# Turning the first half of x by a transposing DMA instead of on TensorE, in front of the e block

## The reference

```python
x = first_block(x, ...)                 # ends in rms_norm(h, final_norm)
for layer in range(2):                  # second block
    h = rms_norm_2(x, g_mix[layer])
    y = even_mixer(h, e_w_in, ...)      # layer 0, "the e block": z = h @ w_in, 2568 columns
    x = x + y
    m = rms_norm_2(mem, g_mem[layer])   # the memory, 256 rows
    x = x + memory_cross_attention(rms_norm_2(x, g_xa[layer]), m, xa_wq, xa_wkv, ...)
    x = x + swiglu_2(rms_norm_2(x, g_ffn[layer]), ...)
```

## Time and profile before

| what | us |
|---|---|
| three runs, median (lowest, highest) | 1207.38 (1206.32, 1207.60) |
| the profiled execution | 1206.72 |
| its span, first to last instruction | 1204.8 |
| TensorE busy in it | 1196.0 |
| VectorE busy | 780.9 |
| ScalarE busy | 701.6 |

### The profile page before, as it was taken

The page is one execution under the profiler, slowest core; times in us unless marked ns, Lnnn a source line. Parts: engine busy times, 40 slices in busy tenths (PEclk is TensorE's granted clock), DMA queues, the critical chain, the costliest instruction groups (busy, mean ns, idle before and its releaser), DMA issues.

```text
span 1204.8 us, 16878 instructions
## 1 busy us (share of the span) xinstructions
PE 1196.0 (99%) x5622; PEld 986.7 (82%) x5622; DVE 780.9 (65%) x1107; ACT 701.6 (58%) x1030; POOL 72.5 (6%) x119
## 2 busy tenths in 40 slices
PE   9999999999999999999999999999999999999998
PEld 7888888877788888887888788888888887888887
DVE  6655655688676656557778766756566667765554
ACT  7545554666556545548676576645555546755552
POOL 0430000000000000000220110000000000000000
PEclk9999999999999999999999999999999999999999
DMA  9977754554566987756655518977655554876662
GB/s 314 275 227 232 231 171 145 170 173 131 166 196 197 280 250 228 220 148 180 201 167 171 167 61 248 267 226 206 206 156 164 160 163 148 237 231 199 202 200 76
DMA packets 218917, 234.68 MB, mean 195 GB/s; under 512 B 66608, under 2 KB 158896, under 8 KB 218864
## 3 DMA queue, kind: packets, MB, share of 16 engines
q1 hardware_dynamic: 163792, 214.61, 57.1%
q10 hardware_dynamic: 53280, 13.64, 6.2%
q0 software_dynamic: 1792, 5.75, 1.8%
HBM read 219.78 MB, written 1.05 MB: 183 GB/s over the span
## 4 chain that ended last, share of the span: by engine, by line
PE 97%; DMA 1%; DVE 1%; ACT 1%; issue 0%; ACTq 0%; DVEq 0%
PE bank L2034 30%; PE bank L2036 30%; PE bank L2035 30%; PE bank L2093 2%; PE bank L2247 1%; PE bank L2263 1%; PE bank L2234 1%; DMA sb_probs<-sb_probs 0%; DMA sb_gates<-h_xT 0%; PE bank L2232 0%; ACT sb_probs L1276 0%; PE bank L2551 0%; DVE sb_rmax L1929 0%; PE bank L2540 0%; PE bank L2265 0%
## 5 line engine op out<-in xcount | busy, mean ns | idle before, releaser
L2034 PE MATMUL bank<-sb_wh,sb_aTh 128*128 128x512 f32 (+1 forms) x1124 | 435.2, 387 | 0.7 <-DVE sb_aTl L1439 0.7
L2036 PE MATMUL bank<-sb_wh,sb_aTl 128*128 128x512 f32 (+1 forms) x1124 | 431.0, 383 | 0.0
L2035 PE MATMUL bank<-sb_wl,sb_aTh 128*128 128x512 f32 (+1 forms) x1124 | 430.7, 383 | 0.0
L1359 DVE TENSOR_TENSOR sb_wl<-sb_raw,sb_wh 128x1024 fp32r<-128x1024 f32 x269 | 325.4, 1222 | 116.5 <-ACT sb_wh L741 111.9
L741 ACT ACTIVATE sb_wh<-sb_raw 128x1024 fp32r<-128x1024 f32 (+1 forms) x275 | 284.5, 1047 | 114.5 <-PE bank L2036 24.8
L2036 PEld LDWEIGHTS bank<-sb_wh,sb_aTl 128*128 128x128 f32 x1124 | 211.2, 188 | 42.0
L2034 PEld LDWEIGHTS bank<-sb_wh,sb_aTh 128*128 128x128 f32 x1124 | 211.3, 188 | 41.7 <-DVE sb_aTl L1439 1.1
L2035 PEld LDWEIGHTS bank<-sb_wl,sb_aTh 128*128 128x128 f32 x1124 | 211.4, 188 | 40.2
L1359 DVE TENSOR_TENSOR sb_wl<-sb_z,sb_wh 128x1024 fp32r<-128x1024 f32 x132 | 160.8, 1224 | 66.7 <-ACT sb_wh L741 66.2
L741 ACT ACTIVATE sb_wh<-sb_z 128x1024 fp32r<-128x1024 f32 x132 | 138.8, 1058 | 76.0 <-PE bank L2036 68.0
L845 ACT ACTIVATE sb_junk<-bank,sb_rstd 128x256 f32<-128x256 f32 x88 | 37.0, 471 | 156.9 <-PE bank L2036 156.6
(11 more groups left out here) (220 smaller groups left out, 928.9 us busy)
## 6 DMA issues: line engine op xcount, KB each, us to landing
sb_raw<-w_in SPq DMA_DIRECT2D x80, 256.0 KB, 3.1
sb_raw<-ffn_w_down SPq DMA_DIRECT2D x60, 256.0 KB, 4.1
sb_raw<-w_down SPq DMA_DIRECT2D x60, 256.0 KB, 4.1
sb_z<-w_gate SPq DMA_DIRECT2D x52, 256.0 KB, 3.3
sb_z<-w_up SPq DMA_DIRECT2D x52, 256.0 KB, 4.1
sb_z<-ffn_w_gate SPq DMA_DIRECT2D x49, 256.0 KB, 3.6
sb_z<-ffn_w_up SPq DMA_DIRECT2D x49, 256.0 KB, 4.4
sb_raw<-e_w_in SPq DMA_DIRECT2D x40, 256.0 KB, 3.1
```

The source lines that it names most:

```text
L1359: dve.tensor_tensor(wl[:, u % NSPLIT, :], raws[SLOT[u]], wh[:, u % NSPLIT, :].bitcast(F32), ALU.subtract).then_inc(low_done, 1)
L2034: pe.matmul(dst, lh, w_hi, start=start, stop=False)
L2035: pe.matmul(dst, lh, w_lo, start=False, stop=False)
L2036: return pe.matmul(dst, ll, w_hi, start=False, stop=stop)
```

## The change

TensorE's call of `xt_half(3, 0)` goes. What ScalarE and VectorE did for the second half of x (planes of 16-bit halves, a transposing DMA, putting the halves together, high part, low part) is now done for each half on its own, with a semaphore for each DMA. The 16-bit planes of half 0 lie in `probs` and those of half 1 in `qkT[3]`; the turned planes go to `probsT` and `qkT[1]`, and the joined x to `qkT[2]` and `qkT[0]`. The lists of ScalarE and VectorE get a new order. The count of turns by TensorE before later norms falls by two (`turns_before`).

```diff
         def turns_before(norm):
-            return 4 * (norm - 1) - (2 if norm > 3 else 0)
+            return 4 * (norm - 1) - (4 if norm > 3 else 0)
...
-            def x3_split():
+            def x3_split(half):
-                act.wait_ge(x_ready, 12)
+                act.wait_ge(x_ready, 10 + 2 * half)
...
-            def x3_turn():
+            def x3_turn(half):
-                act.wait_ge(x3_planed, 1)
+                act.wait_ge(x3_planed, half + 1)
...
-            def x3_high():
+            def x3_high(half):
-                act.wait_ge(x3_joined, 1)
+                act.wait_ge(x3_joined, half + 1)
...
-            splits(mk, 4)
+            splits(mk, 3)
+            x3_split(0)
+            x3_turn(0)
+            split(mk + 3)
             rstd_known(MEM_STAT)
             evac(mk + 4, 0, MEM_STAT, kz[0], memk_evac_a)
-            x3_split()
-            xt_high(3, 0)
-            x3_turn()
+            x3_split(1)
             split(mk + 4)
+            x3_turn(1)
 
             act.wait_ge(small_in, 32)
             copy(wf_hl[:, :, 0:8], wf[:, :, :]).then_inc(wf_high, 1)
             split(mk + 5)
+            x3_high(0)
             token_ssq(3, x)
             split(mk + 6)
             head_squares(kz[0], ((memk_evac_a, 1), (memk_evac_d, 1)))
             split(mk + 7)
-            x3_high()
+            x3_high(1)
             evac(mk + 8, 2, MEM_STAT, vm[0], memv_evac_a)
...
-            xt_low(3, 0)
             split(mk + 4)
+            x3_join(0)
 
             dve.wait_ge(wf_high, 1)
             dve.tensor_tensor(wf_hl[:, :, 8:16], wf[:, :, :], wf_hl[:, :, 0:8].bitcast(F32), ALU.subtract).then_inc(wf_low, 1)
-            splits(mk + 5, 2)
+            split(mk + 5)
+            x3_low(0)
+            split(mk + 6)
             head_sums(0, 3, 4)
-            x3_join()
+            x3_join(1)
             split(mk + 7)
-            x3_low()
+            x3_low(1)
             evac(mk + 8, 2, MEM_STAT, vm[0], memv_evac_d)
...
-            chunk(mk + 4, 2, None, yTh, yTl, before={1: lambda: xt_half(3, 0)})
+            chunk(mk + 4, 2, None, yTh, yTl)
```

More of the change, by code:

```diff
@@ L234, in two_block_kernel @@
                       qkT[:, 1, :, :].rearrange("p h t -> p (h t)").bitcast(U16)]
-        x3_planes = km_planes[0]
-        x3_planesT = km_planesT[0]
-        x3T = qkT[:, 2, :, :]
+        x3_planes = [km_planes[0], qkT[:, 3, :, :].rearrange("p h t -> p (h t)").bitcast(U16)]
+        x3_planesT = [km_planesT[0], km_planesT[1]]
+        x3T = [qkT[:, 2, :, :], qkT[:, 0, :, :]]
         hT_halves = probsT[:, 0, :].bitcast(U16).rearrange("p (k t r h) -> p h k t r", k=2, t=NT, h=2)
@@ L318, in two_block_kernel @@
         x3_planed = sem("x3_planed")
-        x3_turned = sem("x3_turned")
+        x3_turned = [sem(f"x3_turned{half}") for half in range(2)]
         x3_joined = sem("x3_joined")
@@ L796, in load_tables @@
                 act.add_instruction(mybir.InstLoadActFuncSet(name=nc.get_next_instruction_name(), act_func_set_id=number))
-            def x3_split():
-                act.wait_ge(x_ready, 12)
-                halves = x[:, :, 512:1024].bitcast(U16).rearrange("p t (c h) -> p h t c", h=2)
+            def x3_split(half):
+                act.wait_ge(x_ready, 10 + 2 * half)
+                halves = x[:, :, 512 * half:512 * half + 512].bitcast(U16).rearrange("p t (c h) -> p h t c", h=2)
                 for h in range(2):
-                    ins = copy(x3_planes.rearrange("p (h t c) -> p h t c", h=2, t=NT)[:, h], halves[:, h])
+                    ins = copy(x3_planes[half].rearrange("p (h t c) -> p h t c", h=2, t=NT)[:, h], halves[:, h])
                 ins.then_inc(x3_planed, 1)
-            def x3_turn():
-                act.wait_ge(x3_planed, 1)
-                act.dma_start_transpose(x3_planesT.rearrange("p (b r) -> p b r", r=P), x3_planes).then_inc(x3_turned, 16)
-            def x3_high():
-                act.wait_ge(x3_joined, 1)
+            def x3_turn(half):
+                act.wait_ge(x3_planed, half + 1)
+                act.dma_start_transpose(x3_planesT[half].rearrange("p (b r) -> p b r", r=P), x3_planes[half]).then_inc(x3_turned[half], 16)
+            def x3_high(half):
+                act.wait_ge(x3_joined, half + 1)
                 for k in range(4):
-                    col = NORM_FILL[3][1] + 4 + k
-                    copy(aTh[:, 4 + k, :], x3T[:, k, :], vecs[:, col:col + 1]).then_inc(a_high, 1)
+                    col = NORM_FILL[3][1] + 4 * half + k
+                    copy(aTh[:, 4 * half + k, :], x3T[half][:, k, :], vecs[:, col:col + 1]).then_inc(a_high, 1)
             def km_split(l, n_normed):
@@ L1760, in _, with x3_join @@
             evac(mk + 4, 0, MEM_STAT, kz[0], memk_evac_d)
[L1762 to L1766, removed]
+            def x3_join(half):
+                dve.wait_ge(x3_turned[half], 16)
+                turned = x3_planesT[half].rearrange("p (h t k r) -> p h k t r", h=2, t=NT, k=4)
+                halves = x3T[half].rearrange("p k t -> p (k t)").bitcast(U16).rearrange("p (k t r h) -> p h k t r", k=4, t=NT, h=2)
                 for h in range(2):
@@ L1769, in x3_join, with x3_low @@
                 ins.then_inc(x3_joined, 1)
-            def x3_low():
+            def x3_low(half):
                 fill = NORM_FILL[3][0]
[L1774 to L1778, removed]
-            xt_low(3, 0)
+                for k in range(4 * half, 4 * half + 4):
+                    col = NORM_FILL[3][1] + k
+                    dve.wait_ge(a_high, 8 * fill + 1 + k)
+                    dve.scalar_tensor_tensor(aTl[:, k, :], x3T[half][:, k % 4, :], vecs[:, col:col + 1],
+                                             aTh[:, k, :].bitcast(F32), ALU.mult, ALU.subtract).then_inc(a_low, 1)
             split(mk + 4)
+            x3_join(0)
             dve.wait_ge(wf_high, 1)
             dve.tensor_tensor(wf_hl[:, :, 8:16], wf[:, :, :], wf_hl[:, :, 0:8].bitcast(F32), ALU.subtract).then_inc(wf_low, 1)
-            splits(mk + 5, 2)
+            split(mk + 5)
+            x3_low(0)
+            split(mk + 6)
             head_sums(0, 3, 4)
-            x3_join()
+            x3_join(1)
             split(mk + 7)
-            x3_low()
+            x3_low(1)
             evac(mk + 8, 2, MEM_STAT, vm[0], memv_evac_d)
```

## The result

The changed kernel takes 1211.68 us (median of six runs, 1211.06 to 1212.80) against 1207.11 us of the kernel before: 4.57 us slower, ratio 1.004 with the interval 1.003 to 1.005. A second measurement, at the end of the study, gave 1211.24 and the ratio 1.0042 (1.0028 to 1.0056). The forecast was 1208.7 with a range up to 1211.0. The sign that rival C named, an issue of over 2.4 us, is there, and the time is past the range.

The account below looks back on a forecast made before the run. TensorE, holding 97% of the chain, was taken as the bound. The sum -0.92 + 1.85 + 0.17 gave +1.1, plus 0.2 at `forget_sum`: +1.3 us, 1208.7 on the median's scale, range 1206.0 to 1211.0.

Parts of the forecast that it names:

- rival C: ScalarE's queue, planes to fourth split: closely following turns issue or fly longer; +3.3 us for the first, about +4.4 both; chance 0.21.
- The mechanism: E block's third unit: squares behind the wait for join 0 make the low parts 2.0 us late; TensorE waits 1.85 us.
- the DMA traffic: Second pass of 0.52 MB on DMA engines 98% busy: costed at nothing, the e block's splits having over 2 us cover.
- the clock: TensorE around the seam: read at full granted clock, 1.00, the 2.4 GHz level; no term for a fall.
- The saving: TensorE: eight transposes removed, worth 0.92 us, all on the path that sets the end.
- Turn 1's issue: ScalarE's queue, from 565.5 to 566.9: issue of the second transposing DMA, taken at 1.33 us rather than 3.30.
- The first unit: E block's first unit: low parts of blocks 0 to 3 in time, with 1.6 us of cover.
- `forget_sum`: Behind the e block's units: VectorE's copy for it 2.0 us late, adding 0.2 us more.
- The start after a wait: TensorE at the e block's third unit: starting after the wait costs 0.17 us more.

Follow-up runs that it names:

- no_turns_pe: Kernel before, with the eight transposes of x on TensorE left out and nothing in their place: 1206.60 us against 1206.68, ratio 0.9996.
- squares_late: Changed kernel with the two squares of x moved behind the high parts of blocks 4 to 7 on ScalarE: 1209.64 us, kernel before 1206.98.
- one_turn: Changed kernel with the second turn left out, blocks 4 to 7 joined from the first turn's data: 1209.78 us, kernel before 1206.98.
- turn1_in_halves: Changed kernel with the second turn issued as two of half the size: 1209.40 us, kernel before 1206.28.
- extra_turn_before: Kernel before, plus one full-size turn nobody uses, issued by ScalarE where the changed kernel issues its first: 1210.12 us against 1206.28.
- turn1_before_split: Changed kernel with the second turn's issue ahead of the split of the e block's first unit: 1213.42 us, kernel before 1206.68.
- turns_by_sp: Changed kernel, order kept, with both turns issued by SP between the loads of the e block's units: 1210.57 us, kernel before 1206.98.
- changed again: The changed kernel measured once more, unaltered, to see which profile rows repeat: 1211.24 us, kernel before 1206.03, ratio 1.0042.
- order_and_sp: Changed kernel with turns issued by SP and the lists in order of need, `split(mk + 5)` keeping its place: 1209.43 us, kernel before 1206.98.
- ballast3: Kernel before, with three extra VectorE subtractions in front of the low parts of blocks 4 to 7: 1211.64 us against 1206.68.

## Why the prediction was wrong

The mechanism was right, and the sum was short. It put the DMA traffic at nothing, where a late load cost 1.3 us; it took the shorter of two rows for the second issue, where the longer cost 0.6 us; and it had no term for the clock, which cost 1.4 us.

- **The saving (-0.92).** The term was read rightly from the rows, but it is gross. Taken alone it gives 0.51 us at the seam (no_turns_pe), since the next gates bind once TensorE comes earlier.
- **The mechanism (a wait at the e block's third unit, because the squares stand behind the wait for join 0).** Right. The wait is where it was placed, and moving the squares takes 2.0 of its 2.9 us (squares_late).
- **The DMA traffic (costed at nothing, "the splits of the e block's units have over 2 us of cover").** Wrong, and the largest miss before the third unit. The load of the e block's first unit took 4.5 us instead of 2.9. Its split stands 1.1 us earlier in the new list (forecast 565.4, before 566.53), and in front of the second turn and of join 0; it waited 1.14 us, and join 0 came 1.28 us after its forecast. The cover held for TensorE's own need, but not for what stands behind the split.
- **Turn 1's issue (1.33 us).** Wrong, by the choice of the row. I took 1.33 "since it is the row of this place" and gave the 3.30 a small chance. The length goes with the place in the sequence, and turn 1 was the second full-size turn. It took 3.07 us. The prediction's own rule, 0.9 us of idle time in front of `x3_high(0)`, makes that 0.8 us; it cost 0.6.
- **The first unit (1.6 us of cover).** `x3_high(0)` came 1.9 us after its forecast, 1.28 for the load and 0.6 for the issue, so TensorE waited there too, 0.36 us.
- **The clock.** Not in the sum at all: 1.43 us. The rows before showed 1.00 in a stage without waits. They could not show what follows a wait of 2.9 us, and the profiles since show both outcomes.
- **`forget_sum` (+0.2).** Right that it is a near gate; it did not bind in the changed kernel, since VectorE's copy ended at 592.78 and TensorE came at 593.98. It bound in no_turns_pe and in squares_late.

Put together for the profiled execution: TensorE starts the third unit 2.82 us late, which is 0.93 from the forecast's order (-0.92 + 1.85), 1.28 from the load and 0.6 from the issue. The start after a wait (0.13, forecast 0.17) and the clock (1.43) make that 4.38, and the seam is 4.38 longer. The 0.6 has a measurement of its own (one_turn); the 1.28 is read from one profile, and in the second profile of the same kernel join 0 was late by 0.9.

Rival C named the issue and the flight of the turns. Its price for both issues long, 1211.8, lies beside the measured 1211.68, but by luck: the first issue took 1.33, and the time is made up of the load and the clock, which C did not price. The range stopped at C with the first issue long, and ended 0.7 us too low.

What stays open: what it is in the queue that makes the second and third full-size issue long, and what decides whether a wait is followed by the half clock. Neither was settled.

## What to carry to other kernels

Work taken off the bounding engine is worth only what the next gates leave; run the kernel with that work left out before building its replacement. A DMA for which there seems to be room still costs its issue on a queue and the landing time of the loads beside it, so count the cover of each of these loads against the first instruction that stands behind it on its engine, not against the last consumer. Where an edit brings in a wait like these, put the price of a stretch at half clock into the range.

## What the runs showed of the hardware

- The issue of a transposing DMA of 128 x 2048 16-bit elements took 1.33 to 1.35 us or 1.74 to 4.15 us on ScalarE's queue in the same program, by its place in the sequence, and 3.52 to 3.69 us on SP's; those of 128 x 1024 took 1.25 to 1.38 us in all 44 cases of the kernel before, and up to 2.06 us in turn1_in_halves.
- A turn in flight beside a load of 256 KB pieces lengthened that load from 2.9 to 4.5 us, and in extra_turn_before from 3.4 to 5.7 us.
- The granted clock fell to half for 3 to 4 us behind waits of TensorE of 2.41 us (turn1_before_split), 2.50 (extra_turn_before), 2.93 (turns_by_sp, turn1_in_halves, changed again) and 2.94 us (changed), and in order_and_sp after 1.31 us at `forget_sum`; it did not after 2.73 (one_turn) and 2.85 us (ballast3). It can fall when TensorE is at work again: about 1.2 us after the start in turn1_in_halves and extra_turn_before, and 1.5 us after it in the changed kernel's second profile, where that start was at 580.52 and the table has

```profile
581.00:582.00 1.00, 1.00 (x6) 0.80 (x5) 1.00 (x3) 1.00 (x2) 0.17 (x1) 0.99 0.82 285
582.00:583.00 1.00, 1.00 (x4) 0.77 (x3) 1.00 (x2) 0.79 (x1) 0.00 (x0) 0.50 0.48 182
```
